# Expert chunks loaded ahead of the branch weights, with the time mix's tail moved to other buffers

## The reference

```python
p = h @ w_in
y_ret  = retention(q, k, v, g, positions, ret_gn_g)
y_rwkv = rwkv7_time_mix(p_rwkv, ...)      # the "time mix"
y_conv = short_conv(p_conv, conv_w)
gates = sigmoid(h @ w_gate + b_gate)
for i, y in enumerate((y_ret, y_rwkv, y_conv)):
    merged = merged + gates[..., i*d:(i+1)*d] * (y @ w_branch[i])
x = x + gate1 * (merged @ w_o)
h2 = modulate(rms_norm_2(x, norm2_g), shift2, scale2)
x = x + gate2 * hier_moe(h2, ...)         # 32 experts, top 2 of one group
# the end of the time mix
y = head_norm(y, gn_g, eps)
y = y + sum(r * kt * r_k) * v             # the "bonus"
return y * g                              # the "gate"
```

## Time and profile before

| what | value |
|---|---|
| median of 3 runs | 2377.32 us (2377.25 to 2377.35) |
| profiled execution, span | 2375.1 us |
| TensorE busy | 2250.5 us (95%) |
| VectorE, ScalarE, GpSimd busy | 737.4, 411.4, 523.9 us |
| moved by DMA | 654.76 MB, mean 276 GB/s |
| mean granted TensorE clock | 0.992 |

### The profile page before, as it was taken

How to read it: one execution, slowest core, us unless ns; L and a number is a source line. 1 busy time by engine, 2 the same in 40 slices (tenths; PEclk the granted TensorE clock), 3 DMA queues, 4 the chain that set the end, 5 groups by cost and what they waited for, 6 DMA issues and landing times.

```text
span 2375.1 us, 30964 instructions
## 1 busy us (share of the span) xinstructions
PE 2250.5 (95%) x13454; PEld 1516.2 (64%) x13454; DVE 737.4 (31%) x1301; ACT 411.4 (17%) x845; POOL 523.9 (22%) x451
## 2 busy tenths in 40 slices
PE   9999999999999999999988888899999998888887
PEld 8776676686668899888333333378998863333333
DVE  5533224524216755523100000055753221000001
ACT  3320112620103331211000000033112020000001
POOL 2387622257752045000000000012530000000000
PEclk9999999999999999999999999999999999999999
DMA  7377732358751442349999999953332799999998
GB/s 278 109 309 285 304 133 86 129 193 339 303 217 65 138 143 90 107 168 400 425 428 428 428 428 428 416 212 114 121 136 97 283 409 427 427 428 428 428 427 317
DMA packets 136850, 654.76 MB, mean 276 GB/s; under 512 B 9864, under 2 KB 15112, under 8 KB 108168
## 3 DMA queue, kind: packets, MB, share of 16 engines
q1 hardware_dynamic: 136712, 652.72, 69.0%
HBM read 651.64 MB, written 1.05 MB: 275 GB/s over the span
## 4 chain that ended last, share of the span: by engine, by line
PE 73%; DMA 21%; DVE 3%; ACT 1%; issue 1%; SPq 0%; POOL 0%; DVEq 0%; ACTq 0%
PE bank L798 72%; DMA ring<-in_w_exp_up 11%; DMA PRGT<-in_w_exp_up 5%; DMA PRGT<-in_w_exp_down 3%; DMA PRGT<-in_w_exp_gate 1%; ACT R L3378 1%; PE bank L1428 0%; DVE sm L2174 0%; POOL PRGT L3476 0%; SPq L712 0%; DMA ring<-in_hy_w_in 0%; ACT SQ L3418 0%; PE bank L984 0%; DVE PRGT L2652 0%; DVE PRGT L2168 0%
## 5 line engine op out<-in xcount | busy, mean ns | idle before, releaser
L798 PE MATMUL bank<-hT,ring 128*128 128x256 f32 (+1 forms) x2912 | 607.8, 367 | 0.0
L798 PEld LDWEIGHTS bank<-hT,ring 128*128 128x128 f32 x2912 | 521.5, 190 | 81.5 <-issue 15.3
L798 PE MATMUL bank<-PRGT,R 128*32 128x512 f32 x1120 | 278.7, 612 | 27.8 <-DMA PRGT<-in_w_exp_up 16.7
L798 PE MATMUL bank<-ring,R 128*32 128x512 f32 (+1 forms) x992 | 251.2, 587 | 39.0 <-DMA ring<-in_w_exp_up 23.2
L3590 POOL TENSOR_TENSOR SQ<-xT 128x512 f32<-128x512 f32 x4 | 4.2, 1057 | 1187.9 <-DVE xT L2927 1187.7
L798 PE MATMUL bank<-PRGT,ring 128*128 128x256 f32 (+6 forms) x1328 | 223.0, 359 | 0.4 <-ACT PRGT L3133 0.4
L798 PE MATMUL bank<-PRGT,SQ 128*32 128x512 f32 (+2 forms) x864 | 194.6, 530 | 14.4 <-ACT SQ L3418 12.2
L798 PEld LDWEIGHTS bank<-PRGT,ring 128*128 128x128 f32 (+3 forms) x1328 | 186.4, 175 | 32.0 <-issue 3.0
L798 PEld LDWEIGHTS bank<-PRGT,R 128*32 128x32 f32 x1120 | 75.6, 112 | 191.7 <-issue 191.2
L798 PEld LDWEIGHTS bank<-ring,R 128*32 128x32 f32 (+1 forms) x992 | 69.9, 114 | 168.3 <-issue 168.0
L798 PE MATMUL bank<-ring,SQ 128*32 128x512 f32 (+2 forms) x640 | 167.7, 519 | 8.5 <-ACT SQ L3418 8.3
(11 more groups left out here) (427 smaller groups left out, 2491.7 us busy)
## 6 DMA issues: line engine op xcount, KB each, us to landing
PRGT<-in_w_exp_gate SPq DMA_DIRECT2D x42, 2048.0 KB, 31.9
ring<-in_w_exp_up SPq DMA_DIRECT2D x36, 2048.0 KB, 31.9
ring<-in_mlp_w SPq DMA_DIRECT2D x32, 2048.0 KB, 8.9
PRGT<-in_w_exp_down SPq DMA_DIRECT2D x30, 2048.0 KB, 30.9
PRGT<-in_w_exp_up SPq DMA_DIRECT2D x28, 2048.0 KB, 32.1
PRGT<-in_w_ada SPq DMA_DIRECT2D x32, 1536.0 KB, 12.4
ring<-in_w_exp_down SPq DMA_DIRECT2D x24, 2048.0 KB, 33.6
ring<-in_w_exp_gate SPq DMA_DIRECT2D x22, 2048.0 KB, 32.1
```

The costliest lines, as they stand in the source:

```text
L798: return mm(o, lhsT=lhsT, rhs=rhs, start=first, stop=last, **kw)
```

## The change

Four things. `YC` and `YSQ` move from `PR[12:16]` and `SC[24:26]` to `SQ`. GpSimd copies `BV` to `R[0:4]` and `GG` to `R[4:8]`, one COPY of 128x1024 each, and raises `tails_moved` (1 and 2 in each layer); `last_steps` reads the copies. On SP's queue the loads of chunks 0, 1 and 2 and of the first half of `w_o` stand ahead of the three `w_branch` loads instead of behind them; chunk 0 waits for the last time mix product, chunk 2 also for the bonus copy and the conv branch's vector work (`y_conv`), `w_o` for the gate copy. Chunk 3 (slot 6) waits for a new step of `merged`, raised at the third retention sum, in place of the last; so `merged` counts 5 in a layer. The semaphore `c_sig` is folded into `lam_steps`, which makes room for `tails_moved`.

```diff
-        YC, YSQ = [flat(PR[:, 12 + 2 * c:14 + 2 * c, :]) for c in range(TT)], flat(SC[:, 24:26, :])
+        YC, YSQ = [flat(SQ[:, 2 + 2 * c:4 + 2 * c, :]) for c in range(TT)], flat(SQ[:, 0:2, :])
+        BV_LATE, GG_LATE = R[:, 0:4, :], R[:, 4:8, :]
...
-                for q in range(5, 20):
+                for q in range(5, 17):
                     weights(q)
-                sp.wait_ge(sems["branch_done"], l + 1)
-                sp.dma_start(ring[0][:, :].rearrange("p (k n) -> p k n", k=KT),
-                             a["w_o_2"][l][:, 0:512].rearrange("(k p) n -> p k n", p=P)).then_inc(slot_full[0], 16)
...
+                n = BANK_AT[f"rec{l}_1"] + 2
+                sp.wait_ge(bank_full[n % BANKS], filled(n))
+                load_chunk(0)
+                load_chunk(1)
+                sp.wait_ge(sems["tails_moved"], 2 * l + 1)
+                sp.wait_ge(sems["y_conv"], l + 1)
+                load_chunk(2)
+                sp.wait_ge(sems["tails_moved"], 2 * (l + 1))
+                sp.dma_start(ring[0][:, :].rearrange("p (k n) -> p k n", k=KT),
+                             a["w_o_2"][l][:, 0:512].rearrange("(k p) n -> p k n", p=P)).then_inc(slot_full[0], 16)
+                for q in range(17, 20):
+                    weights(q)
                 slot_free = {}
-                slot_free[1] = slot_free[4] = slot_free[5] = (sems["branch_done"], l + 1)
-                slot_free[6] = slot_free[7] = slot_free[8] = (sems["merged"], 4 * (l + 1))
+                slot_free[6] = (sems["merged"], 5 * l + 1)
+                slot_free[7] = slot_free[8] = (sems["merged"], 5 * (l + 1))
...
-                for c in range(MOE_CHUNKS - GROUP_CHUNKS):
+                for c in range(EARLY_CHUNKS, MOE_CHUNKS - GROUP_CHUNKS):
...
                 v.tensor_tensor(flat(cv), flat(cv), flat(PR[:, 34:38, :]), ALU.mult).then_inc(sems["y_conv"], 1)
+                dve.wait_ge(sems["tails_moved"], 2 * (l + 1))
                 step(last_steps(0))
...
+                pool.wait_ge(sems["x_new"], TT * (l + 1))
+                g.tensor_copy(BV_LATE, BV).then_inc(sems["tails_moved"], 1)
+                n = BANK_AT[f"rec{l}_0"] + 2
+                pool.wait_ge(bank_full[n % BANKS], filled(n))
+                g.tensor_copy(GG_LATE, GG).then_inc(sems["tails_moved"], 1)
```

More of the change, by code:

```diff
@@ L370, in build @@
             "ff_full", "ff_read", "ff_act", "asum_ready", "down_done", "combined", "down_turned", "kr_rope", "kr_spread", "q_roped",
-            "c_sig", "ada_loaded0", "ada_loaded1", "ada_summed", "mod_done", "rot_in", "rot_tables", "swapped",
+            "ada_loaded0", "ada_loaded1", "ada_summed", "mod_done", "rot_in", "rot_tables", "swapped",
             "ahead_in", "g_sig", "ret_kq", "ret_norm", "head_var", "head_std",
@@ L374, in build @@
             "v_mixed", "row_ready", "x_new", "rw_norm", "y_conv", "cleared", "branch_done", "merged", "sums_ready", "corner_full", "corner_read",
-            "router_max", "perm_ready", "sq_summed", "route_rstd", "router_exp", "router_w", "moe_sig",
+            "tails_moved", "router_max", "perm_ready", "sq_summed", "route_rstd", "router_exp", "router_w", "moe_sig",
             "assigned", "over_found", "over_known", "sel_ready", "selw_ready", "xs_full", "xs_read_v", "xs_read_a", "swt_full", "swt_read",
@@ L1409, in dense_half @@
                         if p == OUT_PAIR and h == 0 and k % 2 == 0:
-                            pe.wait_ge(sems["merged"], 4 * l + k // 2 + 1)
+                            pe.wait_ge(sems["merged"], 5 * l + k // 2 + 2)
                         ins = mul(acc[b][:, h * S:(h + 1) * S], W[:, k, (2 * j + h) * P:(2 * j + h + 1) * P], rhs(k), k == 0, k == K - 1)
@@ L2114, in _ @@
             dve.wait_ge(sems["vec_chain"], L.up())
-            dve.wait_ge(sems["lam_steps"], 3)
+            dve.wait_ge(sems["lam_steps"], 4)
             v.tensor_tensor(sm[:, LIN:LIN + 4], sm[:, LIN:LIN + 4], sm[:, LAM:LAM + 4], ALU.add).then_inc(sems["vec_chain"], 1)
@@ L2120, in _ @@
             v.tensor_scalar(sm[:, LIN:LIN + 4], sm[:, LIN:LIN + 4], 4.0, None, ALU.mult).then_inc(sems["lam_steps"], 1)
-            dve.wait_ge(sems["c_sig"], L.nxt("c_sig"))
             v.tensor_tensor(sm[:, CS:CS + 8], sm[:, CS:CS + 8], V_("c"), ALU.mult).then_inc(sems["vec_chain"], 1)
@@ L2687, in last_steps @@
                         ins = v.scalar_tensor_tensor(YB[:, 4 + m, cs], o[:, m * P:(m + 1) * P], layer_vec(f"rw_gn{l}", m),
-                                                     BV[:, m, cs], ALU.mult, ALU.add)
+                                                     BV_LATE[:, m, cs], ALU.mult, ALU.add)
                     emptied_bank(n, ins)
                     read_by(n)
-                    return v.tensor_tensor(YB[:, 4:8, cs], YB[:, 4:8, cs], GG[:, :, cs], ALU.mult)
+                    return v.tensor_tensor(YB[:, 4:8, cs], YB[:, 4:8, cs], GG_LATE[:, :, cs], ALU.mult)
                 r0 = BANK_AT[f"rec{l}_0"]
@@ L2749, in branch @@
                             ins.then_inc(sems["merged"], 1)
+                        elif j == 2:
+                            ins.then_inc(sems["merged"], 1)
+                            dve.wait_ge(sems["merged"], 5 * l + 1)
                         else:
@@ L3017, in _ @@
             f(lam, lam, ACT.Ln, bias=1.0).then_inc(sems["lam_steps"], 1)
-            f(sm[:, CS:CS + 8], V_("c"), ACT.Sigmoid).then_inc(sems["c_sig"], 1)
+            f(sm[:, CS:CS + 8], V_("c"), ACT.Sigmoid).then_inc(sems["lam_steps"], 1)
             copy_out(BANK_AT["hy_yr0"], flat(PR[:, YR:YR + 2, :]))
@@ L3030, in _ @@
             th, den = flat(PR[:, RG:RG + 4, :]), flat(R[:, 4:8, :])
-            act.wait_ge(sems["lam_steps"], 4)
+            act.wait_ge(sems["lam_steps"], 5)
             for m in (g0, g0 + 1):
```

## The result

| | median | runs |
|---|---|---|
| before | 2377.45 us (2376.61 to 2379.11) | 20 |
| after | 2381.84 us (2380.67 to 2384.07) | 20 |

The ratio is 1.0018, with a 95% interval of 1.0011 to 1.0024: the change costs 4.4 us. The forecast was 2380.3, with a range of 2376.0 to 2385.0. The profiled execution after has a span of 2380.5 us, 5.4 above that of the earlier trace rows.

The account below looks back on a forecast made before the run. TensorE bounds each layer up to the first expert round, then the chunk stream from chunk 10. Wait 3.0 plus copy 1.0 minus gain 1.0 gives +3.0 us on 2377.3: 2380.3 us, range 2376.0 to 2385.0.

Parts of the forecast that it names:

- What sets the end: In each layer, TensorE sets the end up to the first expert round, the stream of chunks from chunk 10 afterwards.
- The rival of a sooner stream: Expert stream set by when the first chunks are loaded: 42.9 us less, 2334.4 us; chance 0.06.
- The wait for weights(17): Ahead of the branch products, TensorE waits for the first w_branch matrix: 1.2 us layer 0, 1.8 layer 1, sum 3.0.
- the two measured sets: Five loads back to back behind the third w_branch matrix before the change: 27.5 us in layer 0, 26.1 in layer 1.
- The estimate from the Trainium skill: Five loads ending with weights(17) take 24.1 us, landing at 1042.3 in layer 0, so no wait there; not used in the sum.
- The bonus copy: GpSimd's BV copy after the last column sums holds VectorE's head norm, delaying TensorE's masks: 0.5 us per layer, 1.0 together.
- The gain at chunk 10: At the start of the expert stream, chunk 10 and those behind come up to 0.7 us sooner: 1.0 us gained in all.
- the call of no change: Whole kernel: +3.0 us is under 0.2% (4.75 us), so the same, on the slow side; chance of the same 0.67.
- Hidden parts: Gate copy hidden by VectorE's idle time before last_steps; earlier chunk 3, YC/YSQ buffers, folded c_sig and new merged step at nothing.

Follow-up runs that it names:

- both edits: Changed kernel with the bonus copy held behind rec0's third step and the first w_branch load put third, behind chunks 0 and 1: 2377.65 us, ratio 0.9999 to before.

## Why the prediction was right, and where it was off

**What sets the end.** Right: TensorE up to the first expert products, then the stream from chunk 10 on. That the early loads bring nothing is shown by the run with both edits, that the stream starts at chunk 10 by the run that holds it back. From the issue of chunk 10 in layer 1 to the end of the span it is 442.2 us before, 442.3 after (issue at 1938.24), 442.4 with both edits and 442.2 with chunk 10 held back. The rival of a sooner stream, 2334.4 us, is refuted.

**The wait for weights(17).** Mechanism right, shown by the run that takes loads from ahead of it and the two that add one. The term was 3.0 us and measured 3.8. In layer 1 the estimate of 1.8 met 1.7 (the `w_gate` block landed at 1820.29 + 9.3, the matrix at 1839.69 + 15.7, five loads in 25.8 us). In layer 0 it was 1.2 and is 2.07: most of the difference is the `w_gate` block ahead, which landed after 8.4 us and not 7.9; five loads took 27.0 us, 0.2 above the middle of the two measured sets that I took (26.8), and TensorE began 0.12 us after the landing. The estimate from the Trainium skill ("DMA: Bandwidth & Descriptors", section "Where 436 GB/s comes from") of 24.1 us would have given no wait in layer 0. The trace does not agree: the measured 27.0 us, 5.4 for a load of 2 MB, decide.

**The bonus copy.** Mechanism right, shown by the run that holds it back; 1.0 us predicted, 0.9 measured. The copy took 1.04 us, as the one-input row said, and VectorE's scaling, which takes 0.69 us alone, ended 0.54 us after the copy: nearly all of it came behind the copy. By that the trace agrees with the Trainium skill ("SBUF — State Buffer", section "Who interferes with whom").

**The gain at chunk 10.** Wrong. The step "With the backlog gone chunk 10, and every chunk behind it, comes up to 0.7 us sooner" took the landing of one `w_gate` block on an empty queue (7.9 us) for that of a chunk. With the backlog gone chunk 10 of layer 0 landed after 8.5 us in the changed kernel and 8.7 with both edits, where it took 8.6 behind the backlog. In layer 1, for which the prediction had no row, it landed after 8.0 us in the kernel before, 8.2 in the changed one and 8.0 with both edits. And the stream behind it took as long as before, as the stretches of 442.2 to 442.4 us show. The term is about 0, not 1.0. Why a load of 2 MB lands after 7.9 us in one place and 8.7 in another is not shown.

**The sum.** 3.8 + 0.9 + 0 = 4.7 against 4.4 by the medians and 3.0 forecast; the two terms that were off both pointed upwards. The result, 1.0018, lies just inside the 0.2% within which I called it no change, and its interval reaches to 1.0024: that the call of no change held is in part luck, since the two terms were off the same way.

**Hidden parts.** Right: the gate copy at 992.74 in layer 0, over 25 us before VectorE needs it. The earlier chunk 3, the folded semaphore and the other buffers cost nothing that can be measured: without the wait and the copy beside the head norm the time is that of before.

## What to carry to other kernels

Before a load is moved ahead, ask what the consumer behind it waits for: here the slots were full in time anyway, and the stream was started by TensorE's release of the first slot. Moved past other loads on one queue, it delays each of them by about its own length in a back-to-back series (here 5.4 us for 2 MB), and the first that has less slack than that becomes a wait. Count that in landings of loads back to back from the same trace, since the margin here was under 2 us of 27; and put an idle-looking engine's copy where the vector engine beside it has slack.

## What the runs showed of the hardware

A wait of TensorE can cost more than its length. Ahead of the branch products the granted clock stayed at the full level (2.4 GHz) through idle times of 1.53, 1.90 and 2.62 us; around the end of idle times of 3.20, 4.06 and 4.14 us it fell to half for some microseconds, and the products took 1.7, 2.9 and 1.7 us longer. So 0.5 MB more in the queue cost 0.7 us in one layer (idle for 2.62 in place of 1.90) and 3.4 in the other (3.20 in place of 1.53, and 43.37 in place of 41.68 for the products).

The length of the idle time alone does not decide it: 4.06 us cost more than 4.14. In the expert rounds of the changed kernel TensorE twice did 32 products of the same shape behind the same idle time, the first at the full and the second partly at half the clock (below them a window of each, columns as in the earlier trace rows):

```profile
1183.02 7.06 PE L808 MATMUL bank<-ring,R 128*32 128x512 f32 x32 [2.74 <-DMA ring<-in_w_exp_up]
...
1290.68 8.76 PE L808 MATMUL bank<-PRGT,R 128*32 128x512 f32 x32 [2.73 <-DMA PRGT<-in_w_exp_up]
...
1184.00:1186.00 2.00, 2.00 (x12) 0.60 (x9) 0.00 (x0) 0.00 (x0) 0.00 (x0) 1.00 0.98 418
...
1292.00:1294.00 2.00, 2.00 (x6) 0.49 (x4) 0.00 (x0) 0.00 (x0) 0.00 (x0) 0.50 0.98 418
```

What else decides stays open here. By these rows a wait of about 2.7 us cost either its length alone or 1.7 us more.

A load of 2 MB on an empty queue landed after 7.5 to 9.3 us (before: the first `w_branch` matrix of layer 0 after 7.5, a `w_gate` block after 7.9 in layer 0 and 9.2 in layer 1), while five back to back took 25.8 to 27.5 us, 5.2 to 5.5 for each. One load's landing time is no price for another's.
